# A two-block float32 network on one core: GpSimd's last low part in each transition waits for VectorE's sum of squares

## The chip, the core and the metric

The kernel runs on one core of a Trainium2 chip. A core has TensorE (PE in the profile, with its weight loads as PEld), VectorE (DVE), ScalarE (ACT), GpSimd (POOL) and a queue engine that starts DMA transfers (SP). Each has its own instruction stream; they wait for each other through semaphores. The metric is the time of one execution on the device in microseconds (us); lower is better.

## The reference

Two transformer-like blocks, one behind the other, on 512 tokens (528 in the first, which puts 16 meta tokens in front) of width 1024, in float32:

```python
h = h + 0.5 * rmsnorm(swiglu(rmsnorm(h, gn[0]), ffn_w_in[i, 0], ffn_w_out[i, 0]), gn[1])
u = rmsnorm(h, gn[2])
y = mlstm_mixer(u, a_w_in[j], a_conv_w[j], a_conv_b[j], a_gate_b[j], a_w_out[j])
h = h + rmsnorm(y, gn[3])
h = h + 0.5 * rmsnorm(swiglu(rmsnorm(h, gn[4]), ffn_w_in[i, 1], ffn_w_out[i, 1]), gn[5])
...
h = h + 0.5 * swiglu_2(rms_norm(h, ffn1_norm[l]), ffn1_w_gate[l], ffn1_w_up[l], ffn1_w_down[l])
n = rms_norm(h, mix_norm[l])
...
h = h + jnp.concatenate([a, r], axis=-1) @ w_o[l]
h = h + 0.5 * swiglu_2(rms_norm(h, ffn2_norm[l]), ffn2_w_gate[l], ffn2_w_up[l], ffn2_w_down[l])
return rms_norm(h, final_norm)
```

So there are four feed-forward layers (FFN 0 to 3, inner width 2816) and two mixers: an mLSTM mixer between FFN 0 and FFN 1, and one of attention and retention between FFN 2 and FFN 3. An rmsnorm divides a token by the root of its mean square and multiplies by a gain per channel.

## The kernel before, in words

**Low and high parts.** Activations lie transposed, eight tiles `hT` of 128 channels by the tokens. For nearly float32 accuracy every weight and activation is split into a high part in a reduced float format and a low part, the difference, and a product is three matmuls (high by high, low by high, high by low; `product`, L3145). Weights come in units of 128 x 1024 numbers (512 KB) into four slots: SP loads `raw`, ScalarE writes the high part `whi` (`split_hi`, L701), GpSimd subtracts and writes the low part `wlo` (`pool_lo`, L536), and TensorE waits for `lo_done` before it uses the unit. A slot of `raw` is loaded again when its low part is made.

**A transition.** Between two stages the residual is updated and the next norm prepared. `pool_transition` is GpSimd's side of it and is called three times: from FFN 0 to the mLSTM mixer (the first transition), from the mixer to FFN 1 (the second), and from FFN 1 to FFN 2 (the third). The tokens are taken in two halves so that TensorE can start on the first. For each half and each tile k VectorE writes the scaled output (`wa`, L2500 or L2498), GpSimd adds it to `hT` (L553), ScalarE writes `xhi` (L1062 or L1130) and, in the second half, the square of the tile (`sqbuf`, L1084 or L1150), and VectorE writes `xlo` (L2507). Behind the last `xlo` VectorE adds the eight squares: six adds on L1881 and a seventh on L1891, which raises the semaphore `summed`. For each norm of number `norm_at[...]["summed"]` says how high it stands before.

**TensorE in a transition.** `first_halves` (L3234) multiplies the next stage's units u, u+1 and u+2 with both halves (L3246), with the root of the norm not yet known: it is put in later. The fourth unit, u+3, comes behind with all tokens (L3150). Within it, behind its third tile (behind its second in the mLSTM mixer), stand the column sums (`sum_norm`, L3180), which wait for `summed`. Behind the sums ScalarE takes the root (L714), VectorE the reciprocal (L1863), and TensorE, two tiles later in unit u+3, spreads it over the partitions (L3321, L3323); ScalarE copies it to `rbc` (L779). VectorE's next work waits for `rbc`.

The order in the fourth unit, from `pe_ffn` (the mixer has the like):

```python
def halved(k):
    if k == 3:
        sum_norm(pe, norm, n)
    if k == 5:
        spread(pe, rms)
```

**GpSimd's order.** Each engine's order is written out by hand. In a transition GpSimd makes the low parts of u, u+1 and u+2 between the adds, then the last adds, then the low part of u+3. What follows differs: behind the first transition the low parts of the mixer's next units, which wait for ScalarE alone; behind the second and third the low parts of the FFN's units u+4 to u+7, ahead of which `pool_ffn` already waits for `summed`:

```python
if i in (1, 2):
    pool.wait_ge(norm_s["summed"], norm_at[NORM_OF_FFN[i]]["summed"] + 1)
```

Of the kernel before, what the change touches and what calls it, by code (L numbers as in the profile page):

```python
# [127 lines left out]
def program(nc, dram, out, stop=99):  # L128
# [16 lines left out]
    def sems(stage, names):  # L145
        return {n: ctx.enter_context(nc.semaphore(f"{stage}_{n}")) for n in names}
# [78 lines left out]
    def half_tile(buf, k, half, n):  # L225

        a, b = half_span(n, half)
        return buf[:, k * TOK + a:k * TOK + b]
# [10 lines left out]
    def n_of_out(i):  # L239
        return TOK if i == 0 else SEQ  # L240
# [90 lines left out]
    norm_s, out_s = sems("norm", NORM), sems("out", OUTP)  # L331
# [11 lines left out]
    norm_at = [dict(sq_ready=KD * max(i - 1, 0), summed=max(i - 1, 0), hi_ready=before_norm[i], x_ready=before_norm[i]) for i in range(6)]  # L343
# [188 lines left out]
    def pool_lo(pool, u0, u1):  # L532

        def lo(u, r=0):
            pool.wait_ge(hi_done, SLOTS * r + (u + 1))
            pool.tensor_tensor(wlo[:, u % SLOTS, :], raw[:, u % SLOTS, :], whi[:, u % SLOTS, :].bitcast(F32),  # L536
                               ALU.subtract).then_inc(lo_done, 1)

        whole = (u1 - u0) // SLOTS
        if whole > 0:  # L540
            with pool.Fori(0, whole) as r:
                for j in range(SLOTS):
                    lo(u0 + j, r)
        for u in range(u0 + whole * SLOTS, u1):
            lo(u)

    def pool_res_half(pool, i, half, first, last):

        at, n = KD * half, n_of_out(i)
        for k in range(first, last):  # L550
            pool.wait_ge(res_s["t_ready"], res_at[i]["t_ready"] + at + k + 1)
            h = half_tile(hT, k, half, n)
            pool.tensor_tensor(h, h, half_tile(wa, k % 2, half, n), ALU.add).then_inc(res_s["h_ready"], 1)  # L553

    def pool_transition(pool, i, u, u_next):

        pool_lo(pool, u, u_next + 2)
        pool_res_half(pool, i, 0, 1, 4)
        pool_lo(pool, u_next + 2, u_next + 3)
        pool_res_half(pool, i, 0, 4, KD)  # L560
        pool_res_half(pool, i, 1, 1, KD)
        pool_lo(pool, u_next + 3, u_next + 4)

    def pool_decays(pool):
# [22 lines left out]
    def pool_ffn(pool, i):  # L587
# [3 lines left out]
        if i in (1, 2):  # L591
            pool.wait_ge(norm_s["summed"], norm_at[NORM_OF_FFN[i]]["summed"] + 1)
        pool_lo(pool, u0 + (SLOTS if i in (1, 2) else AHEAD), u0 + 2 * NCONV)
# [67 lines left out]
    def prog_gpsimd(pool):  # L661

        pool.wait_ge(lo_done, 2)
        pool_lo(pool, 2, AHEAD)
        u = pool_ffn(pool, 0)
        pool_transition(pool, 0, u, U_M1)
        pool_transition(pool, 1, U_M1 + SLOTS, FFNS[1]["u0"])
        u = pool_ffn(pool, 1)
        pool_transition(pool, 2, u, FFNS[2]["u0"])
        u = pool_ffn(pool, 2)  # L670
        pool_lo(pool, u, U_M2 + 11 + AHEAD)
        pool_decays(pool)
        pool_lo(pool, U_M2 + 11 + AHEAD, U_M2 + 16 + AHEAD)
        pool.wait_ge(a2["roped"], 9)
        for m in range(4):
            if m < 2:
                pool_lo(pool, U_M2 + 16 + AHEAD + m, U_M2 + 17 + AHEAD + m)
            pool_queries(pool, m)
            if m >= 2:
                pool_lo(pool, U_M2 + 16 + AHEAD + m, U_M2 + 17 + AHEAD + m)  # L680
        pool_lo(pool, U_M2 + 20 + AHEAD, FFNS[3]["u0"] + AHEAD)
        pool_ffn(pool, 3)
# [2449 lines left out]
        dve_final(v)  # L3132

    NORM_OF_FFN = [0, 2, 3, 5]

    def out_bank(i, p, n, half=None):

        if half is not None:
            return ps[:, 4 + p % 2, 0:HW]
        return bank(p % 2 + {1: 2 if p < 2 else 4, 4: 0}[i], n)  # L3140
# [1040 lines left out]
```

## Time and profile before

| | |
|---|---|
| median of 3 runs | 1937.84 us |
| lowest, highest | 1937.84, 1943.92 us |
| the profiled execution's own time | 1942.4 us |
| its span, first to last instruction | 1940.6 us |
| its mean granted TensorE clock | 0.998 |

The profile is of a single execution, 4.6 us slower than the median of the runs; its own time is 1.8 us more than its span. Busy times are sums of the records of an engine; a matmul's record has a modelled end and overlaps the next, so the times at which matmuls start say more than their durations. The granted clock is 1.00 at TensorE's full 2.4 GHz and 0.50 at 1.2 GHz.

### The profile page before, as it was taken

What the parts mean: (1) busy time and instruction counts of PE and PEld (TensorE: products, weight loads), DVE (VectorE), ACT (ScalarE), POOL (GpSimd) and SP (SyncE); (2) the same over time, 40 slices, a digit from 0 to 9 for tenths busy, and PEclk for the clock granted to TensorE, in tenths of its full rate; (3) what the DMA queues carried; (4) which work ended last, traced back from release to release, by engine and by line L of the source; (5) the groups of instructions that cost most, each with busy time, mean ns of one, the idle gap of its engine ahead of it and who ended that gap; (6) DMA issues with size and microseconds to landing.
All of it is one profiled execution on the core that took longest, in us unless ns stands there. A gap on an engine that the chain in (4) does not pass through costs nothing. (4 is left out here: it accounts for less than half of the span.)

```text
span 1940.6 us, 38305 instructions
## 1 busy us (share of the span) xinstructions
PE 1901.8 (98%) x13945; PEld 1749.8 (90%) x13945; DVE 1414.5 (73%) x1940; ACT 1026.6 (53%) x1695; POOL 866.7 (45%) x521
## 2 busy tenths in 40 slices
PE   8999999989999999999999999999999999999998
PEld 8999999987778899989989999997785678999898
DVE  5977697786365877687787777877756548777887
ACT  5566654524324566664466666545336335666643
POOL 3455453634325455552645556254442044555623
PEclk9999999999999999999999999999999999999999
DMA  6233333322312233333423333344321032333332
GB/s 179 66 101 105 93 99 108 93 58 66 109 38 83 74 111 108 103 114 87 120 62 105 105 107 112 92 111 114 75 51 55 1 87 69 115 101 106 109 88 87
DMA packets 344606, 178.05 MB, mean 92 GB/s; under 512 B 18716, under 2 KB 340119, under 8 KB 344495
## 3 DMA queue, kind: packets, MB, share of 16 engines
q1 hardware_dynamic: 342640, 175.46, 31.8%
q8 instruction: 74, 1.21, 0.3%
q10 hardware_dynamic: 1854, 1.07, 0.2%
q14 instruction: 38, 0.30, 0.1%
HBM read 174.42 MB, written 2.10 MB: 91 GB/s over the span
## 5 line engine op out<-in xcount | busy, mean ns | idle before, releaser
L3479 PE MATMUL ps<-xop,whi 128*128 128x256 f32 (+1 forms) x4032 | 720.6, 282 | 8.6 <-DVE sq L2013 6.0
L3479 PEld LDWEIGHTS ps<-xop,whi 128*128 128x128 f32 x4032 | 619.3, 189 | 10.8 <-DVE sq L2013 6.8
L3479 PE MATMUL ps<-xop,wlo 128*128 128x256 f32 (+1 forms) x2016 | 566.5, 281 | 0.0
L536 POOL TENSOR_TENSOR wlo<-raw,whi 128x1024 fp32r<-128x1024 f32 x94 | 234.0, 2498 | 376.9 <-ACT whi L701 366.7
L3479 PEld LDWEIGHTS ps<-xop,wlo 128*128 128x128 f32 x2016 | 381.3, 189 | 0.0
L597 POOL TENSOR_TENSOR wlo<-raw,whi 128x512 fp32r<-128x512 f32 x212 | 277.9, 1322 | 220.8 <-ACT whi L831 220.0
L3417 PE MATMUL ps<-xop,whi 128*128 128x256 f32 (+1 forms) x896 | 213.9, 283 | 2.0 <-DVE hT L2184 2.0
L3150 PE MATMUL ps<-xhi,whi 128*128 128x512 f32 (+2 forms) x624 | 211.3, 368 | 2.4 <-DVE xlo L1871 2.3
L3150 PE MATMUL ps<-xlo,whi 128*128 128x512 f32 (+2 forms) x624 | 204.4, 357 | 0.0
L3150 PE MATMUL ps<-xhi,wlo 128*128 128x512 f32 (+2 forms) x624 | 204.0, 356 | 0.0
L3417 PE MATMUL ps<-hid_r,whi 128*128 128x256 f32 (+1 forms) x768 | 190.1, 282 | 0.9 <-POOL wlo L638 0.9
L638 POOL TENSOR_TENSOR wlo<-raw,whi 128x1024 fp32r<-128x1024 f32 x40 | 103.5, 2596 | 167.4 <-ACT whi L971 167.2
L597 POOL TENSOR_TENSOR wlo<-stage,whi 128x512 fp32r<-128x512 f32 x72 | 94.2, 1308 | 178.4 <-ACT whi L831 178.4
L831 ACT ACTIVATE whi<-ps 128x512 fp32r<-128x512 f32 x180 | 107.8, 599 | 107.9 <-DVE ps L1982 81.2
L3417 PE MATMUL ps<-xop,wlo 128*128 128x256 f32 (+1 forms) x576 | 162.3, 282 | 0.0
L2002 DVE TENSOR_TENSOR wlo<-ps,whi 128x512 fp32r<-128x512 f32 x180 | 123.2, 685 | 48.0 <-ACT whi L831 47.6
L3417 PEld LDWEIGHTS ps<-xop,whi 128*128 128x128 f32 x896 | 155.6, 189 | 2.8 <-DVE hT L2184 2.4
L3417 PEld LDWEIGHTS ps<-hid_r,whi 128*128 128x128 f32 x768 | 135.9, 188 | 1.6 <-issue 1.4
L3150 PEld LDWEIGHTS ps<-xhi,whi 128*128 128x128 f32 (+1 forms) x624 | 109.9, 188 | 27.6 <-issue 6.0
L831 ACT ACTIVATE whi<-raw 128x512 fp32r<-128x512 f32 x216 | 134.2, 621 | 0.0
L701 ACT ACTIVATE whi<-raw 128x1024 fp32r<-128x1024 f32 x96 | 99.8, 1050 | 63.2 <-PE ps L3150 49.2
L3150 PEld LDWEIGHTS ps<-xlo,whi 128*128 128x128 f32 (+1 forms) x624 | 110.4, 188 | 18.2 <-issue 2.2
(471 smaller groups left out, 3966.5 us busy)
## 6 DMA issues: line engine op xcount, KB each, us to landing
raw<-in_ffn_w_in SPq DMA_DIRECT2D x88, 512.0 KB, 3.8
raw<-in_ffn_w_gate SPq DMA_DIRECT2D x44, 512.0 KB, 3.8
raw<-in_ffn_w_up SPq DMA_DIRECT2D x44, 512.0 KB, 3.8
raw<-in_ffn_w_out SPq DMA_DIRECT2D x32, 512.0 KB, 4.3
raw<-in_ffn_w_down SPq DMA_DIRECT2D x32, 512.0 KB, 4.3
raw<-in_a_w_in SPq DMA_DIRECT2D x24, 512.0 KB, 3.9
raw<-in_w_in SPq DMA_DIRECT2D x19, 512.0 KB, 3.9
raw<-in_ffn_w_out SPq DMA_DIRECT2D x16, 384.0 KB, 3.5
```

The costliest lines, as they stand in the source:

```text
L536: pool.tensor_tensor(wlo[:, u % SLOTS, :], raw[:, u % SLOTS, :], whi[:, u % SLOTS, :].bitcast(F32), ALU.subtract).then_inc(lo_done, 1)
L597: pool.tensor_tensor(operand(wlo, i, name), source, operand(whi, i, name).bitcast(F32), ALU.subtract) \
L638: ins = pool.tensor_tensor(to, source, down_operand(whi, i, d, block).bitcast(F32), ALU.subtract)
L701: act.activation(whi[:, s, :], raw[:, s, :], ACT.Copy).then_inc(hi_done, 1)
L831: ins = act.activation(operand(whi, i, name), source, ACT.Copy)
L2002: v.tensor_tensor(operand(wlo, i, name), sum_place(i, name), operand(whi, i, name).bitcast(F32), ALU.subtract).then_inc(s["w_lo_dve"], 1)
L3150: ins = pe.matmul(o, lhs[l], x[r], start=first and n == 0, stop=last and n == 2)
L3417: ins = pe.matmul(ps[:, bank_, 0:h], weights[l][:, k * P:(k + 1) * P], parts[r][:, k % 4, :], start=start and k == 0 and q == 0, stop=k == ...
L3479: ins = pe.matmul(to, w[l][:, k * P:(k + 1) * P], x[r][:, k * h:(k + 1) * h], start=start and k == 0 and q == 0, stop=k == 3 and q == 2, s ...
```

## The change

In `pool_transition`, ahead of the low part of unit u+3, GpSimd waits until VectorE has finished the sum of squares of the norm that the transition prepares. Nothing else is changed; `NORM_OF_RES` says which norm that is.

```diff
@@ -559,6 +559,8 @@
         pool_lo(pool, u_next + 2, u_next + 3)
         pool_res_half(pool, i, 0, 4, KD)
         pool_res_half(pool, i, 1, 1, KD)
+        norm = NORM_OF_RES[i]
+        pool.wait_ge(norm_s["summed"], norm_at[norm]["summed"] + 1)
         pool_lo(pool, u_next + 3, u_next + 4)
 
     def pool_decays(pool):
@@ -3132,6 +3134,7 @@
         dve_final(v)
 
     NORM_OF_FFN = [0, 2, 3, 5]
+    NORM_OF_RES = [1, 2, 3]
 
     def out_bank(i, p, n, half=None):
```

GpSimd's instructions at the first transition (128x1024 on L536 is a low part, 128x264 on L553 an add of half the tokens to the residual; in brackets the semaphores that an instruction waits for; - is before, + is the changed kernel):

```order
 L536 TENSOR_TENSOR wlo<-raw,whi 128x1024 [waits hi_done] x2
 L553 TENSOR_TENSOR hT<-hT,wa 128x264 [waits res_t_ready] x3
 L536 TENSOR_TENSOR wlo<-raw,whi 128x1024 [waits hi_done]
 L553 TENSOR_TENSOR hT<-hT,wa 128x264 [waits res_t_ready] x11
-L536 TENSOR_TENSOR wlo<-raw,whi 128x1024 [waits hi_done]
+L536 TENSOR_TENSOR wlo<-raw,whi 128x1024 [waits hi_done,norm_summed]
 L541 UNCONDITIONAL_BRANCH
 L541 ISA
```

No instruction changes its place; the low part of u+3 has a second wait. The same engine at the third transition (the second reads alike):

```order
 L536 TENSOR_TENSOR wlo<-raw,whi 128x1024 [waits hi_done]
 L553 TENSOR_TENSOR hT<-hT,wa 128x256 [waits res_t_ready] x11
-L536 TENSOR_TENSOR wlo<-raw,whi 128x1024 [waits hi_done]
+L536 TENSOR_TENSOR wlo<-raw,whi 128x1024 [waits hi_done,norm_summed]
 L541 UNCONDITIONAL_BRANCH [waits norm_summed]
 L536 TENSOR_TENSOR wlo<-raw,whi 128x1024 [waits hi_done] x4
```

Here the wait for `summed` stood one instruction later before, ahead of the four low parts of the FFN; now it stands ahead of that of u+3 as well.

## Rows read from the trace of the kernel before

**Rows 1.** The page's first part: busy us, share of the span, instructions.
```profile
PE 1901.8 (98%) x13945; PEld 1749.8 (90%) x13945; DVE 1414.5 (73%) x1940; ACT 1026.6 (53%) x1695; POOL 866.7 (45%) x521
```

**Rows 2.** TensorE's waits, whole span: us in total, times, longest us.
```profile
PE ps L3479 <- DVE sq L2013: 6.0, 4, 1.7
PE ps L3180 <- DVE sqbuf L1891: 5.9, 3, 4.9
```

**Rows 3.** Timeline of POOL, first transition: start us, us, instruction, [idle before].
```profile
387.81 2.62 POOL L536 TENSOR_TENSOR wlo<-raw,whi 128x1024 fp32r<-128x1024 f32 x1
393.93 5.12 POOL L536 TENSOR_TENSOR wlo<-raw,whi 128x1024 fp32r<-128x1024 f32 x2 [3.50 <-ACT whi L701]
```

**Rows 4.** Timeline of DVE, first transition.
```profile
388.62 2.11 DVE L2507 SCALAR_TENSOR_TENSOR xlo<-hT,vec,xhi 128x264 fp32r<-128x264 f32 x1 [0.45 <-ACT xhi L1062]
390.65 6.21 DVE L1881 TENSOR_TENSOR sqbuf<-sqbuf 128x528 f32<-128x528 f32 x6
396.89 2.73 DVE L1891 TENSOR_TENSOR sqbuf<-sqbuf 128x528 f32<-128x528 f32 x1
```

**Rows 5.** Timeline of PE, first transition.
```profile
393.05 0.48 PE L3150 MATMUL ps<-xhi,whi 128*128 128x264 f32 x2
...
394.34 0.40 PE L3150 MATMUL ps<-xhi,wlo 128*128 128x264 f32 x2
399.67 2.29 PE L3180 MATMUL ps<-ones,sqbuf 128*128 128x1 f32 x10 [4.93 <-DVE sqbuf L1891]
...
405.72 0.55 PE L3150 MATMUL ps<-xhi,whi 128*128 128x264 f32 x2
```

**Rows 6.** Windows: stretch, length, PE, PEld, DVE, ACT, POOL busy, clock, DMA, GB/s.
```profile
398.00:400.00 2.00, 0.33 (x2) 0.33 (x2) 1.62 (x1) 0.00 (x0) 1.05 (x1) 0.76 0.31 18
404.00:406.00 2.00, 2.00 (x11) 1.72 (x11) 0.00 (x0) 0.00 (x0) 0.00 (x0) 0.54 0.03 8
676.00:680.00 4.00, 2.38 (x21) 2.18 (x19) 3.83 (x6) 1.90 (x4) 1.08 (x2) 1.00 0.46 131
```

**Rows 7.** Timeline of POOL, third transition.
```profile
978.32 2.62 POOL L536 TENSOR_TENSOR wlo<-raw,whi 128x1024 fp32r<-128x1024 f32 x1
985.98 9.45 POOL L536 TENSOR_TENSOR wlo<-raw,whi 128x1024 fp32r<-128x1024 f32 x4 [5.04 <-DVE sqbuf L1891]
```

**Rows 8.** Timeline of DVE, third transition.
```profile
978.20 0.48 DVE L2507 SCALAR_TENSOR_TENSOR xlo<-hT,vec,xhi 128x256 fp32r<-128x256 f32 x1 [0.44 <-ACT xhi L1062]
979.12 2.10 DVE L2507 SCALAR_TENSOR_TENSOR xlo<-hT,vec,xhi 128x256 fp32r<-128x256 f32 x1 [0.44 <-ACT xhi L1062]
...
985.13 0.69 DVE L1891 TENSOR_TENSOR sqbuf<-sqbuf 128x512 f32<-128x512 f32 x1
987.26 0.18 DVE L1863 RECIPROCAL rcol<-rcol 128x4 f32<-128x4 f32 x1 [1.44 <-ACT rcol L714]
...
996.73 1.22 DVE L1944 TENSOR_TENSOR xop_f<-xop_f 128x1024 f32<-128x1024 f32 x1
```

**Rows 9.** Timeline of PE, third transition.
```profile
983.07 0.39 PE L3150 MATMUL ps<-xhi,whi 128*128 128x512 f32 x1
...
984.93 0.39 PE L3150 MATMUL ps<-xhi,wlo 128*128 128x512 f32 x1
985.87 1.05 PE L3180 MATMUL ps<-ones,sqbuf 128*128 128x1 f32 x8 [0.56 <-DVE sqbuf L1891]
...
988.62 0.48 PE L3150 MATMUL ps<-xhi,whi 128*128 128x512 f32 x1
```

**Rows 10.** Timeline of DVE, second transition.
```profile
632.79 2.10 DVE L2507 SCALAR_TENSOR_TENSOR xlo<-hT,vec,xhi 128x256 fp32r<-128x256 f32 x1 [0.44 <-ACT xhi L1130]
```

**Rows 11.** Timeline of PE, second transition.
```profile
636.87 0.39 PE L3150 MATMUL ps<-xhi,whi 128*128 128x512 f32 x1
...
639.54 0.61 PE L3180 MATMUL ps<-ones,sqbuf 128*128 128x1 f32 x4 [0.43 <-DVE sqbuf L1891]
```

**Rows 12.** Timeline of PE in FFN 1, behind the second transition.
```profile
679.90 0.50 PE L3479 MATMUL ps<-xop,whi 128*128 128x256 f32 x2 [1.62 <-DVE sq L2013]
```

## The prediction

> **What bounds the kernel now.** I read the page's busy shares first. TensorE is busy for 98% of the span [rows 1], so a change counts only where it lengthens or shortens one of TensorE's few waits. Then I read TensorE's waits, longest first. The one this change aims at is the wait of the column sums (L3180) for VectorE's last add (L1891): 5.9 us in three times, of which one is 4.9 [rows 2]. Those three are the three transitions. Then the timelines of GpSimd, VectorE and TensorE side by side in each.
>
> In the first transition GpSimd makes the low part of u+3 from 387.81 to 390.43 [rows 3]. VectorE's last xlo starts inside it, at 388.62, and takes 2.11 us [rows 4], where the same operation on nearly the same size takes 0.48 in the clear [rows 8]: it ends just behind GpSimd's. Two more low parts run from 393.93 to 399.05 [rows 3], and VectorE's seven adds from 390.65 to 399.62 [rows 4] take 8.97 us. In the third transition the seven adds, from the end of the xlo at 981.22 to 985.82, take 4.60 us with GpSimd idle [rows 7, 8]. So an add or an xlo on VectorE that meets a low part of GpSimd stands still until that ends. In the first transition three low parts delay the sum; in the second and third only one does, since the next four wait for the sum already [rows 7].
>
> **The change, part by part.** It adds no instruction, only a wait, so the costs are all in what waits for what. The times are those of the profiled execution.
>
> First transition. The last xlo would end at 388.62 + 0.49 = 389.11. The seven adds at 528 instead of 512 tokens: 4.60 x 528/512 = 4.74, which gives a sum at 393.85 instead of 399.62. Now no low part may start before it. That of u+3 starts 0.16 behind (985.82 to 985.98 in [rows 7, 8]) at 394.0 and takes 9.45/4 = 2.36 us in the clear [rows 7], to 396.4. But TensorE needs it: unit u+3 started at 393.05 [rows 5], and its matmuls wait for lo_done. It starts at 396.4 now, 3.35 us later. It has two tiles to do ahead of the sums. From 393.05 to the sixth group of matmuls at 394.34 and one more pitch of 0.26 is 1.55 us, so the sums, which are ready by then, start at 396.4 + 1.55 and some 0.1 of restart, at 398.0, instead of 399.67. Gain: 1.7 us. TensorE's wait here is no longer for the sum but for the low part, 3.4 us instead of 5.1.
>
> Third transition. The last xlo ends at 979.60, 1.62 earlier, and the sum at 984.20. The low part of u+3 runs from 984.36 to 986.72 instead of 978.32 to 980.94 [rows 7]. Before, TensorE started the unit at 983.07 without a wait [rows 9]. Now it stands until 986.77, 3.7 us. Its three tiles ahead of the sums take nine matmuls at (984.93 - 983.07)/8 = 0.233 us, 2.1 in all: the sums would have started at 985.17 but waited to 985.87 [rows 9], 0.7 us. Now they start at 988.87. Loss: 3.7 - 0.7 = 3.0 us. The second transition has the same pattern: its xlo of 2.10 us ends at 634.89 [rows 10] and the sums follow at 639.54 [rows 11], 4.65 us on as in the third (981.22 to 985.87); so the sum comes at 637.87 in place of 639.49, the low part ends at 640.39, and TensorE, which started at 636.87 [rows 11], starts at 640.44: 3.57 us of new wait, less 639.54 - 638.97 = 0.57 of old one, 3.0 us.
>
> What is queued behind the waiting instruction. GpSimd's next low parts, u+4 to u+7, end 0.9 us later (five of 2.36 from 984.36 end at 996.2, against 995.43 [rows 7]), while TensorE comes to them 3 us later, so nobody waits. VectorE's next operation with two operands in SBUF, L1944 at 996.73 [rows 8], depends on rbc and moves by 3 us, so it stays clear of them. SP's reload of the slot of u+3 starts 5.8 us later; unit u+7 is three units of TensorE away. ScalarE's root and all of VectorE's work in the FFN hang on the sums, so they shift with TensorE. I therefore let none of the 3.0 us be won back. The bound on the other side is that TensorE's next wait for VectorE, 1.62 us at 679.90 [rows 12], one in each FFN [rows 2], takes it up: then a transition costs 3.0 - 1.62 = 1.4. I take 3.0, since VectorE is the one waited for there and is itself late by 3.0.
>
> Sum of the waits: -1.7 + 3.0 + 3.0 = +4.3 us.
>
> The clock. In the first transition TensorE stands still from 394.74; in the 2 us from 398 to 400 the granted clock is 0.76, so that it stood at 0.50 for the last 0.96 of them, and from 404 to 406 it is 0.54, so that it was back at 1.00 for the last 0.16 [rows 6]. The level fell from 2.4 to 1.2 GHz at 399.04, behind 4.3 us of standing still, and came back at 405.84. From the start of the sums to the matmul behind the spread TensorE took 405.72 - 399.67 = 6.05 us [rows 5]. At the full clock the third transition takes 988.62 - 985.87 = 2.75 for eight sums [rows 9]; with ten, the longer tiles and the extra spread I estimate 3.1. So the fall cost 2.95 us. A wait of 1.62 us left the clock at 1.00 (676 to 680) [rows 6, 12]. What a wait of 3.4 to 3.7 us does, no row shows: nearest above is 4.93, where it fell, nearest below 1.62, where it did not. Bounds: it falls behind none of the three new waits, and 2.95 us are given back; or behind all of them, and 5.9 are added. I take a clock that costs as much as before, once in the program.
>
> The Trainium skill (TensorE: Matmul & The Clock Gate, "HAM oscillation — how this bites in real kernels") says that an array which waits long enough between bursts of matmuls is put back to the slow clock, so that the next burst starts cold. That speaks against this change, which makes two long waits out of short ones. By that rule alone, every transition would fall, and the sum would be that of the second rival below.
>
> A second rule could add to it. The reciprocal on L1863 reads and writes SBUF, and in the third transition it ran at 987.26 for 0.18 us in the middle of GpSimd's low parts [rows 7, 8]; it is on the path from sums to rbc, and low parts run beside it in both kernels. The skill (SBUF — State Buffer, "SBUF: two separate sides") counts VectorE's two-port modes among what an operation of GpSimd locks out for its whole length, which for such an operation would be up to 2.36 us in a transition. The row shows no lock, and I put it at nothing.
>
> **How this stands to the time.** The profiled execution has 1942.4 us of its own, 1.8 over its span; with +4.3 it would have 1946.7, and with the clock given back 1943.8. It is 4.6 us above the median of the runs, 1937.84, of which one of three was at 1943.92, so the median is the better base: 1937.84 + 4.3 = 1942.1. This is +0.22%.
>
> **Rivals.**
>
> The clock is given back (first rival): no new wait is long enough. For it: all three are shorter than the 4.3 us behind which it fell. Against: the median may hold runs in which it did not fall before, so that there is nothing to give back. 4.3 - 2.95 = +1.35, 1939.2 us.
>
> The clock falls oftener (second rival, slower): the waits at 637 and 983 reach 3.6 and 3.7 us, and behind one or both the matmuls run at 1.2 GHz as they did behind 399 us. Price 2.95 each: 4.3 + 2.95 = +7.3 (1945.1) or 4.3 + 5.9 = +10.2 (1948.0). It decides as soon as one of the waits leaves a stretch of lower clock. For it: 3.7 is nearer to 4.3 than to 1.62. Against: the first transition's own fall came only at the end of its wait.
>
> The loss is small and the gain is larger (third rival, faster): the waits of 1.6 us in FFN 1 and 2 take up part of each loss, the clock comes back, and the mixer behind the first transition gains more than its 1.7 us because VectorE starts there earlier. -1.7 - 2.95 + 2 x 1.4 = -1.85; it passes -0.3% only if the mixer gives 4 us more, for which I see no wait.
>
> The change does nothing: the low part would be late anyway. Against: the low part starts at 387.81 and 978.32, each well before the sum [rows 3, 7]. Time 1937.8.
>
> **Chances.** What a measurement of this kernel can tell from no change is about 0.3%, 5.8 us. Forecast (waits alone, the clock as dear as before) 0.42; clock given back 0.15; clock falls oftener 0.30; losses partly taken up 0.08; nothing 0.05. Slower by over 0.3%: 0.27 of the second rival and 0.14 of the forecast, which lies only 1.5 us below the bound, 0.41. Faster by over 0.3%: 0.05. Within: 0.54. The range of 8 in 10 goes from just under the no-change time to both falls: 1937.0 to 1948.5. The forecast's own range is 1940.5 to 1944.
>
> **What would show it.** In the first transition the sum ends near 393.9 and L3180 starts near 398.0. In the second and third, TensorE has a new wait of about 3.6 us on L3150 for GpSimd's low part (L536), and the wait of L3180 for L1891 is gone in all three. The granted clock of the stretches behind those waits tells the forecast from the rivals. The prediction is wrong in its mechanism if VectorE's adds stay slow with GpSimd idle, or if TensorE's wait on L3150 at the second and third is under 2 us; in its size, if a later wait of TensorE shrinks by as much.

## The result, and the profile after

| | before | after |
|---|---|---|
| median of 8 runs | 1938.32 us | 1951.9 us |
| lowest, highest | 1936.78, 1944.7 us | 1947.43, 1955.05 us |
| ratio, 95% interval | | 1.0064, 1.005 to 1.0078 |
| profiled execution, own time | 1942.4 us | 1951.77 us |
| its span | 1940.6 us | 1950.0 us |
| its mean granted clock | 0.998 | 0.995 |

The change makes the kernel slower by 0.64%. The forecast was 1942.1 us, and the range ended at 1948.5.

The page's first part, which answers to [rows 1]: TensorE's records have 6.8 us more for the same instructions, and VectorE's have 8.8 us less.

```profile
PE 1908.6 (98%) x13945; PEld 1756.4 (90%) x13945; DVE 1405.7 (72%) x1940; ACT 1026.6 (53%) x1695; POOL 865.1 (44%) x521
```

TensorE's waits (us in total, times, longest). This one is new, and the column sums no longer wait for VectorE's last add [rows 2] at all:

```profile
PE ps L3153 <- POOL wlo L536: 8.8, 3, 3.4
```

In the changed kernel the numbers of code lines behind L561 are two higher, and those behind L3134 three higher: L3153 is L3150 of before, L3183 is L3180. In the kernels below that insert two lines only, these two are L3152 and L3182.

**First transition.** VectorE's timeline, which answers to [rows 4]:

```profile
389.00 0.49 DVE L2509 SCALAR_TENSOR_TENSOR xlo<-hT,vec,xhi 128x264 fp32r<-128x264 f32 x1 [0.45 <-ACT xhi L1064]
389.41 4.04 DVE L1883 TENSOR_TENSOR sqbuf<-sqbuf 128x528 f32<-128x528 f32 x6
393.49 0.71 DVE L1893 TENSOR_TENSOR sqbuf<-sqbuf 128x528 f32<-128x528 f32 x1
```

GpSimd's, which answers to [rows 3], and TensorE's, which answers to [rows 5]:

```profile
394.27 7.00 POOL L536 TENSOR_TENSOR wlo<-raw,whi 128x1024 fp32r<-128x1024 f32 x3 [6.05 <-DVE sqbuf L1893]
```

```profile
396.69 0.81 PE L3153 MATMUL ps<-xhi,whi 128*128 128x264 f32 x2 [2.02 <-POOL wlo L536]
...
399.49 1.44 PE L3183 MATMUL ps<-ones,sqbuf 128*128 128x1 f32 x10
...
402.99 0.48 PE L3153 MATMUL ps<-xhi,whi 128*128 128x264 f32 x2
```

The collisions are gone. The last xlo takes 0.49 instead of 2.11 us, the seven adds end at 394.20 instead of 399.62, and the low part of u+3 starts 0.07 us later. Where the sums had waited 4.93 us, TensorE now waits 2.02 us for the low part. The forecast had 3.35: TensorE came to the unit 22.24 us after the transition's start instead of 20.99, since its clock had fallen at 376.2 us, where it had not in the profiled execution of before.

**Second and third transition.** TensorE's timeline in the second, then the third, beside [rows 9, 11]:

```profile
637.54 0.49 PE L3153 MATMUL ps<-xhi,whi 128*128 128x512 f32 x1 [3.32 <-POOL wlo L536]
...
640.35 1.70 PE L3183 MATMUL ps<-ones,sqbuf 128*128 128x1 f32 x8
...
991.09 0.79 PE L3153 MATMUL ps<-xhi,whi 128*128 128x512 f32 x1 [3.44 <-POOL wlo L536]
...
994.58 0.95 PE L3183 MATMUL ps<-ones,sqbuf 128*128 128x1 f32 x8
...
997.23 0.48 PE L3153 MATMUL ps<-xhi,whi 128*128 128x512 f32 x1
```

From the unit's start to its sums the third transition took 985.87 - 983.07 = 2.80 us with the sums' wait in it; it takes 994.58 - 991.09 = 3.49 now, without one. The unit is late, and then runs slower. The windows say why; their columns are those of [rows 6], and the number behind the busy times is the granted clock:

```profile
396.00:398.00 2.00, 1.31 (x6) 1.31 (x7) 0.00 (x0) 0.49 (x1) 2.00 (x2) 0.66 0.08 17
398.00:400.00 2.00, 2.00 (x12) 2.00 (x11) 0.00 (x0) 0.00 (x0) 2.00 (x2) 0.50 0.83 245
...
640.00:646.00 6.00, 6.00 (x22) 5.16 (x21) 0.18 (x1) 0.55 (x2) 4.48 (x2) 0.52 0.72 211
990.00:994.00 4.00, 2.92 (x7) 2.34 (x8) 0.00 (x0) 0.00 (x0) 4.00 (x3) 0.57 0.42 126
```

Behind each of the three new waits TensorE runs at 1.2 GHz. By windows cut ever finer the clock stood at 0.50 for 3.4 us from 396.6, 6.8 us from 639.0 and 3.4 us from 990.6. The forecast had one such stretch.

**Where the time went.** Each transition can be cut at four starts of matmuls: the first of `first_halves`, the first of u+3, the sums, and the first behind the spread. In the profiled execution of before, the first transition starts at 372.06, so the parts are 393.05 - 372.06, 399.67 - 393.05 and 405.72 - 399.67 [rows 5]. In us:

| | first transition | second | third |
|---|---|---|---|
| before, profiled | 20.99 + 6.62 + 6.05 = 33.66 | 20.29 + 2.67 + 2.74 = 25.70 | 20.21 + 2.80 + 2.75 = 25.76 |
| after, profiled | 24.26 + 2.80 + 3.49 = 30.55 | 23.78 + 2.81 + 4.98 = 31.57 | 23.82 + 3.50 + 2.64 = 29.96 |
| difference | -3.1 | +5.9 | +4.2 |

That is 7.0 of the 9.4 us between the spans. The matmuls of FFN 1 between the second and third transition take 1.4 us more (320.57 to 321.94), of which the lower clock, back at 1.00 from 645.8 us on, can only explain the first half microsecond; all behind the third takes 0.8 more, and all ahead of the first 0.4. These also vary between executions of one kernel (below). Against the medians, 13.6 us are to be explained, and the profiled execution of before is not one that lies at its median. That is the second half of the study.

### The profile page after: what moved, and what is told of

Its sections match the earlier page's. It is cut to its first block and busy times, and to the rows that moved or that the text cites. A ratio compares the mean times of both kernels' runs of the same rounds, so it can differ in the third digit from the quotient of the medians.

```text
span 1950.0 us, 38308 instructions
## 1 busy us (share of the span) xinstructions
PE 1908.6 (98%) x13945; PEld 1756.4 (90%) x13945; DVE 1405.7 (72%) x1940; ACT 1026.6 (53%) x1695; POOL 865.1 (44%) x521
## 3 DMA queue, kind: packets, MB, share of 16 engines
q1 hardware_dynamic: 342640, 175.46, 31.5%
## 5 line engine op out<-in xcount | busy, mean ns | idle before, releaser
L3482 PE MATMUL ps<-xop,whi 128*128 128x256 f32 (+1 forms) x4032 | 722.8, 282 | 8.5 <-DVE sq L2015 5.8
L3482 PEld LDWEIGHTS ps<-xop,whi 128*128 128x128 f32 x4032 | 621.3, 189 | 10.6 <-DVE sq L2015 6.6
L3482 PE MATMUL ps<-xop,wlo 128*128 128x256 f32 (+1 forms) x2016 | 568.5, 282 | 0.0
L536 POOL TENSOR_TENSOR wlo<-raw,whi 128x1024 fp32r<-128x1024 f32 x94 | 232.6, 2483 | 383.8 <-ACT whi L703 365.9
L3482 PEld LDWEIGHTS ps<-xop,wlo 128*128 128x128 f32 x2016 | 380.0, 188 | 0.0
L3153 PE MATMUL ps<-xhi,whi 128*128 128x512 f32 (+2 forms) x624 | 213.3, 371 | 11.2 <-POOL wlo L536 8.8
L3153 PE MATMUL ps<-xlo,whi 128*128 128x512 f32 (+2 forms) x624 | 205.8, 359 | 0.0
L3153 PE MATMUL ps<-xhi,wlo 128*128 128x512 f32 (+2 forms) x624 | 205.3, 358 | 0.0
L3153 PEld LDWEIGHTS ps<-xhi,whi 128*128 128x128 f32 (+1 forms) x624 | 110.8, 189 | 36.9 <-POOL wlo L536 9.4
L3153 PEld LDWEIGHTS ps<-xlo,whi 128*128 128x128 f32 (+1 forms) x624 | 111.5, 190 | 18.4 <-issue 2.2
```

The costliest lines, as they stand in the source:

```text
L3153: ins = pe.matmul(o, lhs[l], x[r], start=first and n == 0, stop=last and n == 2)
L3482: ins = pe.matmul(to, w[l][:, k * P:(k + 1) * P], x[r][:, k * h:(k + 1) * h], start=start and k == 0 and q == 0, stop=k == 3 and q == 2, s ...
```

## The experiments

Unless it says otherwise, each kernel is the kernel before with the edit shown, and none of the edits changes the output. The filler matmuls of some kernels write a PSUM bank that the next unit overwrites, and nothing reads them. "Mean" is the difference of the mean times of a kernel and of before on the same chip. The median comes first, then the ratio with its 95% interval.

**The wait in the first transition alone.**

```diff
+        if i == 0:
+            pool.wait_ge(norm_s["summed"], norm_at[i + 1]["summed"] + 1)
         pool_lo(pool, u_next + 3, u_next + 4)
```

> The wait for the sum of squares stands ahead of the low part of u+3 in the first transition only. Theory (waits plus clock): the column sums there start about where they did in the changed kernel, some 1.7 us earlier than in the kernel before by the waits, and the clock falls there in both, so -1 to -3 us against the kernel before: 1936 to 1937. Rival (the first transition carries part of the loss too, by a clock that falls oftener): no gain or +3 us.

1942.43 us, 1.0004 (0.9991 to 1.0018), mean +0.8. First transition 30.45 us. The gain read from the profile was 33.66 - 30.45 = 3.2 us; the runs show none. The clock did not fall at the start here, and TensorE waited 3.30 us for the low part, as forecast; the transition is as long as with the fall, since the low part sets when the unit starts.

**In the second and third alone** (`if i in (1, 2):`).

> The wait stands in the second and third transition only. Theory: two new waits of TensorE of 3.3 to 3.6 us for the low part of u+3, each with a clock that falls behind it: 2 x 3.0 for the waits and 2 x 2 to 3 for the clock, +10 to +12 us against the kernel before. Rival (waits alone, the clock as before): +6 us. Rival (the changed kernel's loss comes from somewhere else): under +4 us.

1954.1 us (7 runs; the others have 12), 1.0061 (1.004 to 1.0081), mean +11.0. The loss is here. In its profile the second transition takes 29.96 and the third 30.01 us, with stretches of clock 0.50 of 3.4 us from 638.5 and 990.1.

**The changed kernel with the waits filled.** Ahead of the wait for the low part of u+3, 24 (first transition) or 15 matmuls keep TensorE busy.

```diff
+            if m == 3:
+                keep_warm(pe, bank(0, TOK)[:, 0, :], 0, HALF, 24)
             pe.wait_ge(lo_done, u0 + m + 1)
...
+            if between is halved:
+                keep_warm(pe, p[0][0], META, SEQ, 15)
             pe.wait_ge(lo_done, r * 4 + (u + 1))
```

> The changed kernel, with TensorE doing matmuls that nobody reads (15 of 512 columns in the second and third transition, 24 of 264 in the first) while it waits for the low part of u+3. They end about when the low part does, so the waits cost the same and only the clock differs. Theory (half of the loss is the clock): the granted clock stays at 1.00 behind the three waits, and the time falls by 6 to 8 us against the changed kernel, to 1943 to 1946, +4 to +7 against the kernel before. Rival (the loss is the waits alone, larger than forecast): the time stays within 2 us of the changed kernel's 1952.

1946.91 us, 1.003 (1.0018 to 1.0041), mean +5.3, where the changed kernel's 8 runs had a mean of +11.6: half of the loss is gone. The same windows of this kernel:

```profile
640.00:646.00 6.00, 6.00 (x30) 4.92 (x30) 3.43 (x7) 2.57 (x4) 4.55 (x3) 1.00 0.73 212
990.00:994.00 4.00, 4.00 (x25) 3.44 (x24) 0.18 (x1) 0.86 (x2) 4.00 (x3) 1.00 0.79 231
```

The second transition takes 28.73 us: +3.0 against 25.70, the loss that was forecast for the wait, and the other 31.57 - 28.73 = 2.8 us of the changed kernel are the clock's. The first takes 29.93 and the third 29.51 us, only 0.6 and 0.5 less than in the changed kernel. From the unit's start on they take 1.6 and 1.4 us less (1.46 + 3.24 against 2.80 + 3.49, and 2.08 + 2.65 against 3.50 + 2.64), but the unit starts later: the fillers outlast the low part by 1.0 us in the first and 0.3 in the third, where the clock also fell early, at 967.4 us.

**The same without the first transition's part** (the kernel with the wait in the second and third, 15 fillers in each).

> The wait ahead of u+3's low part in the second and third transition only, as in the earlier run of that, with 15 unread matmuls of 512 columns in TensorE's wait there. Theory: the waits alone, 2 x 3.0 us: +6 us against before, 4 to 6 us faster than the same without the matmuls. Rival (the clock is no large part): +9 to +11 as without them.

1948.05 us, 1.003 (1.0017 to 1.0044), mean +6.4, where the two waits without fillers had +11.0: the fillers give back 4.6 us, by runs on two chips. Second transition 28.69 us. The first, which this kernel leaves as it was, takes 33.65 us in the profile, with its sum's wait of 4.92; that execution took 1952.18 us and lies in the upper half of the 12 runs (six from 1944.2 to 1947.0, six from 1949.1 to 1952.8).

**The kernel before, unchanged.**

> The kernel before, unchanged, for its granted clocks. Theory: its clock falls behind the 4.9 us wait of the first transition in every run, and what parts its runs at 1937 from those at 1944 is one or two further falls. Rival: the fast runs are those in which the clock did not fall there. Time 1937 to 1944, ratio 1.00.

1941.78 us, 1.0005 (0.9989 to 1.002), mean +0.9. Over the three chips of these experiments the kernel before, as the other side of each comparison, had 94 runs, in two groups: on one, 15 runs lie from 1936.6 to 1939.6 and 14 from 1942.9 to 1947.7, with none between; on the others 18 of 30 and 20 of 35 lie in the lower group. The 12 runs here are less clean: five up to 1940.0, two at 1941.6 and 1941.9, five from 1944.0 on. The profiled execution of before (1942.4 us) and the one here (1944.6 us) both take 33.66 us for the first transition and leave open what the lower group does.

**The wait behind the low part of u+3, in the first transition.** The low part comes early as before, and only those of u+4 and u+5 wait for the sum.

```diff
         pool_lo(pool, u_next + 3, u_next + 4)
+        if i == 0:
+            pool.wait_ge(norm_s["summed"], norm_at[i + 1]["summed"] + 1)
```

> The kernel before, with the wait for the sum of squares in the first transition only and behind the low part of u+3, so that it holds back the mixer's next two low parts alone. Theory (an add of VectorE that meets a low part stands still; TensorE pays only if its own low part is held): the sum ends 4.1 us earlier, at about 395.5, TensorE's wait for it falls from 4.9 to about 0.9 us, the clock does not fall there, and the time is 4 to 7 us under the kernel before. Rival (what delays the sum is ScalarE or the adds themselves): no difference over 1 us.

1938.28 us, 0.998 (0.9969 to 0.9991), mean -3.4: faster than both kernels, by less than the 4 to 7 us that were expected. All 12 runs lie from 1936.8 to 1940.7; the upper group is gone. GpSimd's timeline, then TensorE's:

```profile
388.15 2.61 POOL L536 TENSOR_TENSOR wlo<-raw,whi 128x1024 fp32r<-128x1024 f32 x1
...
395.98 4.75 POOL L536 TENSOR_TENSOR wlo<-raw,whi 128x1024 fp32r<-128x1024 f32 x2 [5.22 <-DVE sqbuf L1893]
```

```profile
393.39 0.48 PE L3152 MATMUL ps<-xhi,whi 128*128 128x264 f32 x2
...
395.80 1.28 PE L3182 MATMUL ps<-ones,sqbuf 128*128 128x1 f32 x10 [0.73 <-DVE sqbuf L1893]
...
399.14 0.48 PE L3152 MATMUL ps<-xhi,whi 128*128 128x264 f32 x2
```

TensorE starts u+3 at once, waits 0.73 us for the sum, keeps its clock, and is through in 26.72 us.

**The same again,** on another chip.

> The version with the wait behind the low part of u+3 in the first transition only, once more, to see whether its 3 us hold beside a fresh set of runs of before: ratio 0.998, and under both filled kernels, since it shortens the wait where they only fill it. Rival (its first result was chance): ratio 1.000.

1938.04 us, 0.9983 (0.9969 to 0.9997), mean -3.2. First transition 27.09 us. In this profile the clock fell at the transition's start (376.2 us), in the first it did not (26.72): with the wait behind the low part both executions are short.

**The low part of u+3 earlier still**, ahead of GpSimd's last seven adds, in all three transitions.

```diff
+        pool_lo(pool, u_next + 3, u_next + 4)
         pool_res_half(pool, i, 1, 1, KD)
-        pool_lo(pool, u_next + 3, u_next + 4)
+        if i == 0:
+            pool.wait_ge(norm_s["summed"], norm_at[i + 1]["summed"] + 1)
```

> As the run with the wait behind the low part in the first transition, and in all three transitions the low part of u+3 moved ahead of the seven last adds of GpSimd, where GpSimd stood idle for 2.4 us. Theory: it no longer meets the last xlo, so the sum ends another 1.6 us earlier in each and TensorE's waits of 0.9 and twice 0.6 us go: 1 to 2 us under the other run. Rival: it meets VectorE's xlo operations of the first half and delays GpSimd's adds, and TensorE waits there instead: slower than the other run by 1 to 5 us.

1940.32 us, 0.9992 (0.9982 to 1.0003), mean -1.3. First transition 27.26 us; the second takes 26.52 instead of 25.7, since the adds, and with them the `xlo` tiles that TensorE waits for, come later (2.3 us of such waits in the second transition, 1.1 before). It gives back some of what the last version won; the theory, 1 to 2 us under it, missed.

**The kernel before with the first transition's wait filled:** 38 matmuls of 264 columns ahead of the sums.

```diff
             if k == 2:
+                keep_warm(pe, ps[:, 6, 0:HALF], 0, HALF, 38)
                 sum_norm(pe, 1, TOK)
```

> The kernel before, with 38 matmuls of 264 columns that nobody reads in TensorE's 4.9 us wait for the sum of the first transition. The wait stays, the clock stays at 1.00 behind it. Theory: 3 us faster than before, by the 2.95 us that the fall cost in the profile; the warm changed kernel at 1946.9 is then 7 to 8 us slower than this one, which would be the price of the waits alone, against 4.3 forecast. Rival (a fall costs little): within 1 us of before, and the waits alone are worth 5.

1942.81 us, 1.0001 (0.9991 to 1.0011), mean +1.1.

> The kernel before with the sum's wait of the first transition filled, once more, since its first run showed no gain (ratio 1.0001) where its profile showed 3.3 us less between the sums and the spread. Theory (the first result was chance): ratio 0.998 to 0.999. Rival (what the clock gives back there is lost elsewhere): ratio 1.000 to 1.001 again, and the profile shows where.

1942.9 us, 1.0002 (0.999 to 1.0014), mean +2.0. The 3 us expected of a kept clock don't come. In both profiles the first transition takes 31.65 us, but that is not the profile of before with the clock kept: in both the clock fell at the transition's start (377.1 and 377.7 us), the first part took 22.3 us, and the 38 fillers ran for their whole time. What the same start takes without them is shown by the profiles below: 27.1 us. So they cost 4.6 us there. How an execution with fast start goes with these fillers is in no profile.

**The first transition's wait ahead of the low part, filled** (24 matmuls).

> The wait ahead of u+3's low part in the first transition only, with 24 unread matmuls of 264 columns in TensorE's wait there. Theory (the first transition gains by its waits, and its clock need not fall): 2 us under the same without the matmuls and 1 to 3 under before, 1938 to 1940. Rival (the clock is not worth it there): as without them, 0 to +1 us.

1941.78 us, 0.9999 (0.9986 to 1.0013), mean +0.4. First transition 29.93 us, 0.5 less than without fillers; the theory's 2 us missed, since the fillers outlast the low part by 1.0 us here as well.

**Two more profiles of the kernel before and two of the changed one.** They ask what the lower group does.

> The kernel before, unchanged, for one more profile. Theory: from the first halves of the first transition to the matmul behind its spread it takes 33.7 us again, with the clock falling behind the 4.9 us wait, and what parts fast from slow executions is the pace of TensorE in the FFNs (320.6 or 321.8 us from the second transition to the third) and further falls. Rival: in fast executions the clock does not fall in the first transition and it takes about 30.7.

> As the look before this one: 33.7 us in the first transition by the theory, 30.7 in a fast execution by the rival.

1940.61 and 1938.8 us; first transition 27.05 and 27.11 us, not 33.66. The first one's VectorE, then GpSimd:

```profile
389.53 2.11 DVE L2507 SCALAR_TENSOR_TENSOR xlo<-hT,vec,xhi 128x264 fp32r<-128x264 f32 x1 [0.45 <-ACT xhi L1062]
391.56 4.04 DVE L1881 TENSOR_TENSOR sqbuf<-sqbuf 128x528 f32<-128x528 f32 x6
395.64 0.71 DVE L1891 TENSOR_TENSOR sqbuf<-sqbuf 128x528 f32<-128x528 f32 x1
```

```profile
388.73 2.62 POOL L536 TENSOR_TENSOR wlo<-raw,whi 128x1024 fp32r<-128x1024 f32 x1
...
396.16 5.29 POOL L536 TENSOR_TENSOR wlo<-raw,whi 128x1024 fp32r<-128x1024 f32 x2 [4.82 <-ACT whi L701]
```

The xlo collides as in [rows 4], but the adds don't: they end at 396.35, and the next low parts start only at 396.16. Those wait for ScalarE's high parts of u+4 and u+5, and ScalarE does these behind an operation that waits for the matmuls of `first_halves` (L3246). ScalarE's timeline in the profiled execution of before, then in this one:

```profile
392.30 0.61 ACT L1431 ACTIVATE E<-ps 128x528 f32<-128x528 f32 x1 [3.17 <-PE ps L3246]
392.81 2.00 ACT L701 ACTIVATE whi<-raw 128x1024 fp32r<-128x1024 f32 x2
```

```profile
394.53 0.61 ACT L1431 ACTIVATE E<-ps 128x528 f32<-128x528 f32 x1 [4.49 <-PE ps L3246]
395.04 2.00 ACT L701 ACTIVATE whi<-raw 128x1024 fp32r<-128x1024 f32 x2
```

The high parts start 0.24 us ahead of the unit u+3 on TensorE in both (393.05 [rows 5], and 395.28 here), so they follow TensorE's progress through `first_halves`. And that goes with the clock at the transition's start, here in windows of before and then of this profile:

```profile
374.00:378.00 4.00, 3.94 (x33) 3.91 (x34) 3.95 (x7) 1.74 (x4) 4.00 (x4) 1.00 0.25 63
378.00:382.00 4.00, 4.00 (x34) 3.94 (x34) 3.57 (x9) 2.35 (x6) 1.55 (x3) 1.00 0.24 72
```

```profile
374.00:378.00 4.00, 3.72 (x28) 3.53 (x28) 4.00 (x6) 1.31 (x4) 4.00 (x4) 0.88 0.04 7
378.00:382.00 4.00, 4.00 (x26) 4.00 (x26) 3.53 (x10) 2.46 (x6) 2.09 (x3) 0.69 0.42 124
```

A fall of the clock at the start makes TensorE 1.3 us slower (22.28 instead of 20.99 us from the transition's start to u+3), the next low parts come behind VectorE's adds, and the sums start without a wait:

```profile
395.28 0.48 PE L3150 MATMUL ps<-xhi,whi 128*128 128x264 f32 x2
...
396.81 1.17 PE L3180 MATMUL ps<-ones,sqbuf 128*128 128x1 f32 x10
...
400.05 0.48 PE L3150 MATMUL ps<-xhi,whi 128*128 128x264 f32 x2
```

So the kernel before has two ways through the first transition: about 27.1 us with a slow start and no collision, and 33.66 us with a fast start, three collisions, a wait of 4.93 us and the clock's fall behind it. All six profiles whose first transition is as of before fit: the clock fell around the start in three (27.05, 27.11 and 28.64 us) and not in the other three (33.66 twice and 33.65). The version with the wait behind the low part is the test: with a fast start it takes 26.72 us, so it is the two low parts that make a fast start long. The two groups of runs lie about as far apart as the two ways, 6.6 us. That each group is one of the ways is read from these profiles, not from every run: the first profile here, on the short way, took 1940.61 us and the profiled execution of before, on the long way, took only 1.8 us more: outside the first transition it was the faster by 4.8 us. The spread of the runs bears it out in the experiments: kernels that leave the first transition alone spread over 8.6 to 11.1 us from lowest to highest, those with a new wait on GpSimd in it over 3.9 to 5.4. The changed kernel doesn't fit, with 7.6 us in its 8 runs; what spreads them was not found.

> The changed kernel, unchanged, for one more profile. Theory: the clock falls behind each of the three waits for the low part of u+3 again, and each of the second and third transition takes 4.2 to 6 us more than before. Rival: the falls in the first profile were chance, and one or two of the three are missing.

> As the look before this one: three falls and 4.2 to 6 us in the second and third transition by the theory, one or two falls by the rival.

1952.46 and 1950.37 us. The three transitions take 30.48, 31.59, 30.01 and 30.55, 31.52, 29.98 us, within 0.1 of the first profile of this kernel, and the clock falls behind all three new waits in both. The clock fell ahead of the first transition in the one (367.3 us) and at its start in the other (375.7 us), and TensorE waited 3.30 and 2.00 us for the low part; the transition is equally long. The changed kernel's first transition has one way only.

**The sum over all kernels.** 53 of 94 runs of before lie in the lower group, so its mean first transition is 0.56 x 27.1 + 0.44 x 33.7 = 30.0 us. Against that, and 25.7 and 26.1 for the other two (the third took 25.76 in one profile of before and 26.4 in three), the transitions of each kernel give, with those that it leaves as they were counted as of before:

| kernel | by its transitions | measured, mean |
|---|---|---|
| the changed kernel (three profiles) | +10.3 | +11.6 |
| wait in the first alone | +0.5 | +0.8 |
| the same, filled | 0.0 | +0.4 |
| before, 38 fillers (two kernels) | +1.7 | +1.1, +2.0 |
| second and third, filled | +6.6 | +6.4 |
| all three, filled | +6.3 | +5.3 |
| second and third | +8.2 | +11.0 |
| wait behind the low part (two kernels) | -3.1 | -3.4, -3.2 |
| low part earlier still | -1.5 | -1.3 |

(The kernels whose profile shows the first transition as of before, 28.6 or 33.7 us, are counted at 30.0 there.) The changed kernel is off by 1.3 us and the two waits alone by 2.8, the others by 1.0 or less. The profile of the two waits alone has the shorter fall in the second transition, 29.96 us, where three profiles of the changed kernel show 31.5; with that it would be +9.8. What it does in its other runs is not known.

## Why the prediction was wrong

**Right: the mechanism of the waits.** A low part on GpSimd holds up VectorE's operations; without it xlo and adds were to take 0.49 and 4.74 us and took 0.49 and 4.79 (389.41 to 394.20). The low part of u+3 was to start behind the sum, and does. The new waits in the second and third transition were to be 3.6 and 3.7 us and are 3.32 and 3.44. With the clock kept, the second transition costs +3.0, as forecast. The price of the fall in the kernel before was to be 2.95 us, and it is 2.8: from the sums to the matmul behind the spread 6.05 us, against 400.05 - 396.81 = 3.24 on the short way. (A small slip changes nothing: by the prediction's own numbers the low parts behind u+3 end 0.8 us later, not 0.9.) Nothing is won back in the FFN: the wait for VectorE on L3482 has 5.8 us in four against 6.0 [rows 2].

**Wrong, first: "a clock that costs as much as before, once in the program".** The clock falls behind all three waits, in each of three profiles. The second rival ("falls oftener") had this mechanism, a chance of 0.30 and 2.95 us for each fall. It cost 2.8 us in the second transition (31.57 - 28.73). In the third it cost about 1.2: 29.96 us, against an estimate of 25.76 + 3.0 = 28.8 with the clock kept (1.4 by the rows of the filled kernel above). Together 4.0 us, where the forecast had none. That a wait of 3.4 to 3.7 us lies between 1.62 and 4.93 was sound as a bound and no ground for a choice. The first transition shows how little a single row at 1.62 excludes: the clock fell there behind waits of 2.02, 2.00 and 3.30 us. The rule that the prediction weighed there (the Trainium skill, TensorE: Matmul & The Clock Gate, "HAM oscillation — how this bites in real kernels": an array that waits long enough between bursts of matmuls starts the next one at the slow clock) is what the runs bear out behind the waits of 3.3 and 3.4 us; by it alone the sum was that of the second rival with both falls, 1948.0.

**Wrong, second: the gain of 1.7 us in the first transition, set against the median.** Against the profiled execution it is larger than forecast: 33.66 - 30.55 = 3.1 us. But only 0.55 of it lies ahead of the sums, since the unit u+3 took 2.80 us to them at the lower clock and not the 1.55 of the forecast; the rest behind the sums shrank from 6.05 to 3.49. The prediction then put its sum on the median, 1937.84, because the profiled run was 4.6 us above it. Above all those 4.6 us come from this very transition: a run of the lower group, in which the median lies, goes through it in about 27.1 us by the two profiles of the short way, has no wait for the sum, and has nothing to win. No run at the median itself was profiled. Against the short way the change costs 30.5 - 27.1 = 3.4 us. The step is off by 1.7 + 3.4 = 5.1 us. The prediction named the doubt ("the median may hold runs in which it did not fall before") but let it touch the clock alone, not the 4.93 us of wait.

**The sum as it should have read:** from a median run of before, +3.4, +5.9, and +3.5 to +4.2 for the third transition (29.96 against 26.4 or 25.76), 12.8 to 13.5 us. Measured: 13.6 between the medians of 8. The forecast's 4.3 plus 4.0 for the clock and 5.1 for the base is 13.4. Part of that agreement is luck: between the means, where before is a mixture of its two ways, the transitions give 10.3 of 11.6 us, and the stretches between them vary by over 1 us from one execution to the next.

**The reciprocal** was put at nothing: right. It again ran beside the low parts for 0.18 us (the VectorE column of the changed kernel's window 640 to 646).

**Why the other place is better.** In the first transition the low part of u+3 collides with one xlo and makes the sum 1.6 us later, of which TensorE waits for at most 0.73 us; the two low parts behind it are those that cost the wait. Made to wait behind u+3, nothing of TensorE's is late, and the kernel goes its short way in both its profiles and, by the narrow spread of its runs, in the rest. In the second and third transition that wait stood there before [rows 7].

## What to carry to other kernels

When the profiled execution lies away from the median, find what makes the difference before costing a change on that spot: take more than one profile, since the wait to be removed may be absent in the usual run. A wait moved ahead of an instruction that the busiest engine needs is paid in full and then again in clock; put it behind that instruction, ahead of the ones that only collide. A wait to be filled with idle matmuls costs their whole time whenever it isn't there.

## What the runs showed of the hardware

- The clock fell behind waits of TensorE of 2.02 and 2.00 us as well as behind 3.3 and 3.4 us (in the first two it had also fallen at the transition's start, and been back at 1.00 for 17 us); the lower level lasted 3.4 us in some cases and 6.8 us in others, for the same place in different executions (638.5 and 639.0 us). Why one or the other was not found.
- It also fell where TensorE hardly waited, at the start of the first transition (375.6 to 377.7 us in nine of the 17 profiles, not in the first of before) and in the first part of the third (962.5 to 973.0 us in nine). What decides that, and so which way the kernel before goes, is open. In the kernel with the wait in the second and third transition it fell there twice, at 368.8 and 379.1, and the first transition took 28.64 us.
- A slower clock early can make a program faster: 1.3 us lost from 376 us on moved two engines' work apart, and the first transition was 6.6 us shorter in all.
- At a granted clock of 1.00 the same matmuls of FFN 1 took 320.5 to 320.9 us in some profiles and 321.6 to 322.2 in others, of the same kernel too (320.57 and 321.75 for before). The cause stays open; it is 1.2 us in a comparison of two single profiles.
